# Two moving halves in one matmul for gate and up, the second mixer's first scores moved into its projections, shared denominators, and a bias canvas filled only in its gaps

## The reference, cut to what matters

```python
def swiglu(h, wg, wu, wd):
    return (jax.nn.silu(h @ wg) * (h @ wu)) @ wd        # wg, wu: 1024 x 2816, wd: 2816 x 1024

# second mixer (layer 0): 16 query heads on 2 key heads, window of 128 keys
dist = pos.reshape(B, nb, BLOCK)[..., :, None] - posb[..., None, :]
bias = rel_bias[t5_bucket(dist)]
scores = jnp.where(valid, scores * scale + bias, NEG)
m = jnp.maximum(jnp.max(scores, axis=-1, keepdims=True), sink)
p = jnp.exp(scores - m)
probs = p / (jnp.sum(p, axis=-1, keepdims=True) + jnp.exp(sink - m))
# third mixer (layer 1): 16 heads of latent attention, plain softmax, no sink
```

## Time and profile before

| what | value |
|---|---|
| median of 3 runs | 1310.5 us |
| profiled execution, its own time | 1308.92 us |
| its span in the trace | 1307.2 us |
| TensorE busy, share of the span | 95% |
| VectorE, ScalarE, GpSimd | 60%, 46%, 10% |
| mean granted clock of TensorE | 0.982 |

### The profile page before, as it was taken

One profiled execution on the slowest core, in us unless ns is written; L12 is line 12 of the kernel. 1 busy time (PEld: TensorE's weight loads), 2 busy tenths in 40 slices (PEclk: granted clock), 3 DMA queues, 4 the chain that ended last, 5 costly groups with the idle time before them and its releaser, 6 DMA issues.

```text
span 1307.2 us, 20632 instructions
## 1 busy us (share of the span) xinstructions
PE 1240.0 (95%) x8470; PEld 1133.7 (87%) x8470; DVE 786.6 (60%) x1019; ACT 603.7 (46%) x786; POOL 135.8 (10%) x165
## 2 busy tenths in 40 slices
PE   6898899999899999979999999999999869999998
PEld 6895799999799999866999999999998757999997
DVE  4787565555575555666755555755555675755554
ACT  5456533333444333566544334543334585543342
POOL 4432100000400000241100000100000430100000
PEclk9898899999999999979999999999999989999999
DMA  9973265556375555451465555565554313555530
GB/s 309 342 203 99 65 212 183 188 188 197 124 249 193 179 179 189 161 165 58 150 204 184 180 183 193 167 192 178 181 177 146 129 33 102 189 188 178 183 127 33
DMA packets 158047, 221.60 MB, mean 170 GB/s; under 512 B 6056, under 2 KB 136172, under 8 KB 157852
## 3 DMA queue, kind: packets, MB, share of 16 engines
q1 hardware_dynamic: 155356, 212.28, 50.6%
q0 software_dynamic: 2624, 8.37, 2.0%
HBM read 213.26 MB, written 7.38 MB: 169 GB/s over the span
## 4 chain that ended last, share of the span: by engine, by line
PE 84%; DVE 8%; ACT 3%; issue 1%; SPq 1%; POOL 1%; DMA 1%; DVEq 0%; ACTq 0%
PE ps L251 27%; PE ps L252 26%; PE ps L253 26%; PE ps L537 2%; DVE w_lo L232 1%; DMA raw<-in_w_in 1%; POOL scratch L780 1%; PE ps L562 1%; PE ps L550 1%; ACT w_hi L225 1%; DVE arena L640 1%; DVE scratch L787 0%; DVE h_lo L426 0%; ACT h_hi L418 0%; SPq L1273 0%
## 5 line engine op out<-in xcount | busy, mean ns | idle before, releaser
L232 DVE TENSOR_TENSOR w_lo<-raw,w_hi 128x2048 fp32r<-128x2048 f32 x194 | 443.2, 2285 | 266.8 <-ACT w_hi L225 266.8
L225 ACT CAST w_hi<-raw 128x2048 fp32r<-128x2048 f32 x197 | 374.2, 1900 | 442.4 <-PE ps L253 430.4
L251 PE MATMUL ps<-h_hi,w_hi 128*128 128x256 f32 x1744 | 495.5, 284 | 7.5 <-DVE h_lo L426 7.5
L253 PE MATMUL ps<-h_hi,w_lo 128*128 128x256 f32 x1744 | 494.1, 283 | 0.0
L252 PE MATMUL ps<-h_lo,w_hi 128*128 128x256 f32 x1744 | 494.1, 283 | 0.0
L251 PEld LDWEIGHTS ps<-h_hi,w_hi 128*128 128x128 f32 x1744 | 335.2, 192 | 11.1 <-issue 6.5
L252 PEld LDWEIGHTS ps<-h_lo,w_hi 128*128 128x128 f32 x1744 | 335.2, 192 | 2.1
L253 PEld LDWEIGHTS ps<-h_hi,w_lo 128*128 128x128 f32 x1744 | 335.1, 192 | 0.0
L251 PE MATMUL ps<-w_hi,act_hi 128*128 128x512 f32 x480 | 187.5, 391 | 1.4 <-DVE act_lo L1012 1.4
L252 PE MATMUL ps<-w_lo,act_hi 128*128 128x512 f32 x480 | 187.4, 390 | 0.0
L253 PE MATMUL ps<-w_hi,act_lo 128*128 128x512 f32 x480 | 186.7, 389 | 0.0
(11 more groups left out here) (230 smaller groups left out, 981.7 us busy)
## 6 DMA issues: line engine op xcount, KB each, us to landing
raw<-in_ffn_wg SPq DMA_DIRECT2D x44, 1024.0 KB, 5.4
raw<-in_ffn_wu SPq DMA_DIRECT2D x44, 1024.0 KB, 5.3
raw<-in_ffn_wd SPq DMA_DIRECT2D x44, 1024.0 KB, 4.9
raw<-in_w_ff SPq DMA_DIRECT2D x32, 1024.0 KB, 5.3
raw<-in_w_in SPq DMA_DIRECT2D x8, 1024.0 KB, 15.4
raw<-in_a_w_in SPq DMA_DIRECT2D x5, 1024.0 KB, 5.3
canvas<-act POOLq DMA_DIRECT2D x6, 688.0 KB, 11.5
raw<-in_w_out SPq DMA_DIRECT2D x4, 1024.0 KB, 6.6
```

Source lines behind the costliest of these rows:

```text
L225: nc.scalar.copy(w_hi[:, b % RING, 0:n], raw[:, b % RAW, 0:n]).then_inc(hi_ready, 1)
L232: nc.vector.tensor_tensor(w_lo[:, b % RING, 0:n], raw[:, b % RAW, 0:n], w_hi[:, b % RING, 0:n].bitcast(F32), ALU.subtract).then_inc(lo_rea ...
L251: nc.tensor.matmul(to, still[0], moving[0], start=start, stop=False, skip_group_check=True)
L253: return nc.tensor.matmul(to, still[1], moving[0], start=False, stop=stop, skip_group_check=True)
```

## The change

- **Wide products.** `h_hi` and `h_lo` become halves of one tile `h_both`. In the SwiGLU stages `wide_features_out` sends both through `w_hi` in one matmul of 512 columns and `h_hi` through `w_lo` in one of 256, where three of 256 stood. The two halves of the result stand side by side in PSUM; `sum_halves` (a VectorE reduce) adds them into SBUF. Gate takes banks 0 and 1, up banks 2 and 3, each a single buffer: TensorE waits for `gate_summed` and `upper_summed` of the step before. `times_row` then reads SBUF, and `act` reads the summed up from SBUF.
- **Row of norms.** Its two matmuls go to bank 4 and stand after the first gate block instead of after the first up block; TensorE waits for the row's copy before the first `second_product` (F0 too).
- **MA.** The first pair's scores stand in the middle of the last query projection. ScalarE copies a turned tile out before it takes the next squares; squares, sums and scaling of the last projection, turns 3 and 4, and rounding and splitting of block `a_in + 7` move into attention steps. Two of the later bias loads stand ahead of POOL's last reciprocal root.
- **Denominators.** `prob_vector` works on a pair: one addition of the sinks and one reciprocal for both heads, behind the exponentials of both.
- **Canvas.** POOL fills only the gaps that no bias covers, out of a small tile `neg`, with four DMAs of 127x8x129 floats and one of 32 single floats. It does so in F0, after `norm_pool(2)`; MA's `bias_load` waits for it, M1 no longer does. The load of `post_gain` moves from behind block 8 to behind block 14.

```diff
-        h_hi = sb("h_hi", [P, KD, TOK], F32R)
-        h_lo = sb("h_lo", [P, KD, TOK], F32R)
+        h_both = sb("h_both", [P, KD, 2, TOK], F32R)
+        h_hi, h_lo = h_both[:, :, 0, :], h_both[:, :, 1, :]
...
+        def wide_features_out(b, bank, turn=0, wait_h=None):
...
+            for f in range(2):
+                for k in range(KD):
+                    if wait_h is not None and f == 0 and k % 2 == 0:
+                        nc.tensor.wait_ge(h_lo_ready, wait_h + k // 2 + 1)
+                    nc.tensor.matmul(ps[:, bank + f, :], hi[:, k, f * P:(f + 1) * P], h_both[:, k, :, :].rearrange("p a b -> p (a b)"),
+                                     start=k == 0, stop=False, skip_group_check=True)
+                    last = nc.tensor.matmul(ps[:, bank + f, 0:TOK], lo[:, k, f * P:(f + 1) * P], h_both[:, k, 0, :],
+                                            start=False, stop=k == KD - 1, skip_group_check=True)
...
+        def sum_halves(to, bank):
+            return nc.vector.tensor_reduce(to.rearrange("p (f t) -> p f t", f=2),
+                                           ps[:, bank:bank + 2, :].rearrange("p f (h t) -> p f t h", h=2), AX.X, ALU.add)
...
-        def prob_vector(h):
-            e = h.e
-            nc.vector.wait_ge(exp_ready, e + 1)
+        def prob_vector(pair):
+            e = pair[0].e
+            both = slice(e % 4, e % 4 + 2)
+            nc.vector.wait_ge(exp_ready, e + 2)
...
         def swiglu_tensor(st, n, s, turn=0):
-            if s >= 2:
-                nc.tensor.wait_ge(hidden_ready[st], s - 1 + 2 * turn)
-            features_out(b_gate(st, s), hidden_bank(s % 2), turn=turn, wait_h=4 * n if s == 0 else None)
+            if s:
+                nc.tensor.wait_ge(gate_summed, steps_ahead[st] + s + 2 * turn)
+            wide_features_out(b_gate(st, s), 0, turn=turn, wait_h=4 * n if s == 0 else None)
+            if s == 0:
+                row_tensor(n)
+            if s:
+                nc.tensor.wait_ge(upper_summed, steps_ahead[st] + s + 2 * turn)
+            wide_features_out(b_upper(st, s), 2, turn=turn)
             if s == 1:
                 nc.tensor.wait_ge(row_ready, FEED[n] + 1)
-            features_out(b_upper(st, s), hidden_bank(2 + s % 2), turn=turn)
-            if s == 0:
-                row_tensor(n)
...
-            times_row(gate[:, s % 2, :], s % 2).then_inc(gate_scaled[st], 1)
+            sum_halves(gate[:, s % 2, :], 0).then_inc(gate_summed, 1)
+            nc.vector.wait_ge(gate_summed, steps_ahead[st] + s + 1 + 2 * turn)
+            times_row(gate[:, s % 2, :], gate[:, s % 2, :]).then_inc(gate_scaled[st], 1)
...
-            nc.gpsimd.memset(act[:, :, :], NEG).then_inc(neg_ready, 1)
-            pool.wait_ge(neg_ready, 1)
-            fill = canvas.rearrange("h n c -> (h n c)").rearrange("(p c) -> p c", p=P)
-            NF = fill.shape[1] // 6
-            for n in range(6):
-                nc.gpsimd.dma_start(fill[:, n * NF:(n + 1) * NF],
-                                    act[:, :, :].rearrange("p a b -> p (a b)")[:, 0:NF]).then_inc(canvas_filled, 16)
+            nc.gpsimd.memset(neg[:, :], NEG).then_inc(neg_ready, 1)
...
-                    if n in (1, 2):
-                        turned_a(n + 2)
+                    if n == 1:
+                        squares_a(4)
+                    if n == 2:
+                        turned_a(3)
+                    if n == 4:
+                        round_block(first["a_in"] + 7)
+                    if n == 5:
+                        turned_a(4)
...
-                               wait_h=16 if p == 0 else None)
+                               wait_h=16 if p == 0 else None, before=(lambda: scores_tensor(heads_a[0:2])) if p == 4 else None)
```

More of the change, by code:

```diff
@@ L568, in pairs_of, with attention_tensor @@
             return [heads[n:n + 2] for n in range(0, len(heads), 2)]
-        def attention_tensor(heads, between=None, after=None):
+        def attention_tensor(heads, between=None, after=None, begun=0):
             pairs = pairs_of(heads)
             for n in range(len(pairs) + 3):
-                if n < len(pairs):
+                if begun <= n < len(pairs):
                     scores_tensor(pairs[n])
@@ L671, in attention_vector @@
                 if 1 <= n <= len(pairs):
-                    for h in pairs[n - 1]:
-                        prob_vector(h)
+                    prob_vector(pairs[n - 1])
         G, H1, HM = 6, 6, 4
@@ L984, in hidden_bank @@
             return lambda f: ps[:, bank, f * TOK:(f + 1) * TOK]
+        upper = carve(3072, 2, 512)
+        gate_summed = sem("gate_summed")
+        upper_summed = sem("upper_summed")
+        steps_ahead = {st: I1 * n for n, st in enumerate(swiglu)}
         def second_product(st, b, s, buf, begin, end, turn=0, per=0):
@@ L1421, in turned_a, with squares_a @@
                                          scale=q_col if p else k_col).then_inc(a_turned_out, 1)
+                def squares_a(p):
+                    if p >= 2:
+                        scalar.wait_ge(a_sums, p - 1)
+                    for t in range(TT):
+                        last = nc.scalar.activation(sq_a[:, p % 2, 256 * t:256 * t + 256], ps[:, 4 + p % 4, 256 * t:256 * t + 256], ACT.Square,
+                                                    scale=token_scale(4, t))
+                    last.then_inc(a_squares, 1)
                 for p in range(5):
@@ L1687, in scale_heads, with sums_a @@
                     last.then_inc(a_scaled, 1)
-                for p in range(5):
+                def sums_a(p):
                     vector.wait_ge(a_squares, p + 1)
@@ L1692, in _ @@
                                             AX.X, ALU.add).then_inc(a_sums, 1)
-                    if p < 4:
-                        split_block(first["a_in"] + p + 3)
+                for p in range(4):
+                    sums_a(p)
+                    split_block(first["a_in"] + p + 3)
                     if p:
                         scale_heads(p - 1)
-                split_block(first["a_in"] + 7)
                 def between_a(n):
                     if n == 1:
+                        scale_heads(3)
+                    if n == 2:
+                        sums_a(4)
+                    if n == 3:
                         scale_heads(4)
+                    if n == 9:
+                        split_block(first["a_in"] + 7)
                     if n == 10:
```

74 lines of the change are left out of this document (44 added, 30 removed).

## The result

The changed kernel takes 1297.73 us (median of 4 runs, 1291.56 to 1299.77) against 1310.57 before (4 runs, 1310.06 to 1314.68); the ratio is 0.9889, interval 0.9865 to 0.9912. That is 13 us less where 25 were forecast, and outside the range. The four times of the changed kernel spread over 8 us, so a few microseconds of one profile are not the kernel's.

What follows compares the result with a forecast made beforehand. TensorE's stream was taken as the bound, busy 95% of the span. Gains of 17.3 + 3.1 + 4.0 + 0.5 = 24.9 us gave a median of 1285.5 us, range 1277 to 1294 (8 in 10).

Steps and rivals of the forecast that it cites:

- Wide products, 17.3 us: SwiGLU stages: each of 1408 triples of matmuls falls from 0.3597 to 0.3474 us, 17.3 us in all.
- `sum_halves` hidden: SwiGLU steps: two reduces of about 1.22 us on VectorE hide behind 11 us of other matmuls; cost 0, bound 3.
- The row of norms: SwiGLU stage entries: moved behind the first gate block, its last diagonal ties with gate's end; at most half a microsecond per stage.
- Rival C: SwiGLU steps: the reduces become the bound and the kernel gets slower, median about 1330 at 4.0 us each; chance 0.03.
- The start, 3.1 us: Kernel start: without the canvas fills a block lands earlier, the split starts 3.1 us earlier, and all behind shifts; bounds 0, 4.6.
- MA's entry, 4.0 us: MA's first attention steps: earlier scores and maxima remove TensorE's wait, second scores up to 5.0 us earlier; 4.0 us, bounds 0, 8.
- rival B: MA's entry or the start gives its gain back, `out_pair` waiting on late rounding or turn 4's copy; median 1290.5, chance 0.15.
- Rival A: SwiGLU stages: the narrow matmul behind a wide one takes what the third took, no 17.3 us; median 1302.9, chance 0.10.
- the 2.5 ns: SwiGLU stages: the skill's fixed part per isolated matmul, by which the wide products would gain only 3.5 us in all.
- Denominators: Attention: 4.6 us of VectorE's reciprocals and additions go, mostly inside its waits; 0.5 us gained, bounds 0 and 2.
- the fill in F0: F0: 2.1 MB of small pieces under block loads cost 0, covered by the ring; without it some 2 us once.

Runs made afterwards that it cites:

- e2: The wide products alone, with the row of norms moved, on top of the kernel before: median 1300.00 us, ratio 0.9919.
- e7: The changed kernel with all 16 wide matmuls of a block first, then its 16 narrow ones: median 1291.92 us, ratio 0.9856.
- e15: The changed kernel with groups of 16 wide, then 16 narrow matmuls, each stage's first feature half still alternating, plus the filler: 1285.44 us, ratio 0.9810.
- e8: The changed kernel with every `sum_halves` done twice, the first result unused: median 1296.09 us, ratio 0.9904.
- e1: The changed kernel run and profiled again, with no edit: median 1296.72 us, ratio 0.9898 to the kernel before.
- e5: The canvas part alone on the kernel before, gaps filled in F0 and no full fill at the start: 1308.62 us, ratio 1.000.
- e6: MA's new entry alone on the kernel before: median 1309.88 us, ratio 0.9990, times in two groups.
- the filler: 11 transposes of a constant, results unused, in TensorE's 1.28 us wait at MB's entry; alone on the kernel before: 1309.97 us, ratio 1.000.
- e4: The changed kernel with each feature half's 8 wide matmuls first, then its 8 narrow ones: median 1294.68 us, ratio 0.9874.
- e3: The changed kernel without the wide products, all else kept: median 1305.08 us, ratio 0.9967, times in two groups.
- e9: The changed kernel with MA's entry as it was before: median 1298.38 us, ratio 0.9901.
- e10: The shared denominators alone on the kernel before: median 1308.26 us, ratio 0.9975.
- e11: The changed kernel with the filler added at MB's entry: median 1291.99 us, ratio 0.9845.
- e13: MA's new entry alone on the kernel before, with the filler at MB's entry: median 1314.00 us, ratio 1.0005, times in two groups.

## Why the forecast was wrong

- **Wide products, 17.3 us: right in mechanism, mis-sized; 9.7 measured by the stages, 10.6 by e2.** The step that failed is "I take 17.3, since both widths were measured with the same kind of weight load in front, in the very stream where they will stand". They were measured in runs of one width. In runs of one width they hold (e7: 0.2269 and 0.1194), and alternating in the first two steps of most stages too, at 0.3468 a pair. In the nine later steps, behind a second product, the same pair takes 0.3528 and not 0.3474, and the second products take 0.2296 and not 0.2275 a matmul. Nor does the first feature half of a stage gain anything, 3.07 us before and after. Steps of 16.57 us in e7 and stages of 186.3 us in e15 are the forecast's numbers, reached by another order alone.
- **`sum_halves` hidden: right.** 1225 ns, no wait of TensorE in the steps, and doubled (e8) it costs 2.5 us by the stages, 1.3 of them in F1 and 1.0 in F2. The thin place was the stage's end, as named: 0.69 us there in e8, nothing in the changed kernel. The row of norms cost nothing: TensorE goes from the first gate block to its two matmuls without a wait. Rival C was far off.
- **The start, 3.1 us: right in M1, not seen in the whole.** ScalarE's wait went; M1 is 1.7 to 2.8 us shorter in three profiles (after, e1, e5), and 2.9 by the medians of 11 profiles with the canvas part against 6 without. e5's ratio of 1.000 lets no more than 2.4 us through. Longer stretches at 0.50 where F0 and F1 begin took some of it back in two of these three profiles, and not in the third.
- **MA's entry, 4.0 us: 6.2 in MA, and nearly nothing at the end.** The second scores came the 5.0 us earlier that were forecast. The rest of the 6.2 goes with the clock in MA: with a stretch left there, as in e6, the stage gives 2.7. Of rival B's signs one was there, `out_pair` waiting 1.30 us for turn 4's copy, but it cost MA far less than MA won. B had the right outcome for the total: where the profiles show the gain gone (after, e6), it went to the clock in MB. That the stretches at the lower clock elsewhere stay as they were was never written down, and the sum rested on it.
- **The new stretch at MB's entry, about 5 us, stood in no term.** It follows an idle time of 1.28 us that every version without the filler has. In profiles without the filler it came in four of the seven with MA's new entry (after, e1, e4, e6; not in e3, e7, e8) and in none of the five without it (before, e2, e5, e9, e10). With the filler it came in none of five (e11 to e15), and e11 is 4.7 us faster than e1. e13 shows that this is no rule for the total: there a loss came some 35 us later instead.
- **Rival A, none of the fixed part saved:** as wrong as the forecast; 9.7 of 17.3 came. The median of 1297.7 lies nearer to A's 1302.9 than to 1285.5, but by MB's loss and not by A's mechanism. By the 2.5 ns of the Trainium skill's "TensorE: Matmul & The Clock Gate", section "Back-to-back issue gap", 3.5 us would have come; the trace has 9.7.
- **Denominators and the fill in F0:** small, as forecast. The prediction gave the fills some 2 us of disturbance once the ring no longer covers them; they slowed F0's block loads from 5.3 to 17.2 us, and the ring covered even that.

The sum after the fact, against the first profile of before: wide 9.7, M1 1.7, MA 6.2, together 17.6; less 6.0 in MB and 1.1 in F0, and 1.3 of F1's gain, is 9.2, which is the difference of the two profiles' spans (1307.2 and 1298.0). e1's profile has 12.9.

**Open:** why the same idle time is followed by a lower clock in one execution and not in the next, and so whether MA's new entry makes it likelier or seven profiles against five show chance. The two groups in the times of e3, e6 and e13 (5, 7 and 8 of 12 in the slower one) speak for a real effect of the new entry, but weakly: of the 93 times of before 18 lie above 1313 as well, and in e13 the slower group can't come from MB's entry. Why the same alternating pair costs 0.3468 us in the first two steps of 22 stages out of 24, and 0.3528 behind the first second product, is open too: TensorE was not idle in either, and the order alone removes it (e4, e7), so alternating widths are part of it and not the whole. e10's gain is open between 1 and 5.5 us.

## What to carry to other kernels

Price a new stream of matmuls from rows in which the same widths follow each other in the same order, and check the price at several places of the loop: here one mixed stream had two prices, and putting one width in a group before the other brought the lower one back by reordering alone. A gain in one stage is not yet a gain in the kernel while the granted clock has stretches at its lower level: compare stage by stage, with the clock beside each, over several executions, before a few microseconds are given to an edit. Where TensorE waits a microsecond between two dense stages, a few matmuls on a constant in that wait are cheap to try, and must be timed in the version that will run.

## What the runs showed of the hardware

- Matmuls with weight loads, at the clock of 2.4 GHz: 0.2269 us per start with 512 columns and 0.1194 with 256 in runs of 16; for the pair when they alternate 0.3468 in the first two steps of a stage and 0.3528 in the later ones (after, F2).
- An idle time of 1.28 us before a stage in which TensorE is then fully busy is followed, some 2 us later, by about 10 us at 1.2 GHz in some executions and not in others: at MB's entry in 4 of 12 profiles, at MA's and F3's, with the same idle time, in none.
- 512 KB to HBM in pieces of 516 bytes took 47.9 us to land, against 11.5 for 688 KB in large ones; block loads of 1 MB beside them took 17.2 us instead of 5.3.
